# A two-layer decoder trunk in split fp32: gated blocks turned in two operations and moved by DMA, and a second seven-product step in gate/up tiles 3 to 9

## The reference

```python
def swiglu(h, w_gate, w_up, w_down):
    return (jax.nn.silu(h @ w_gate) * (h @ w_up)) @ w_down

for i in range(DEPTH):
    h = rms_norm(x, norm_mix[i])
    x = x + (gla_mixer(h, ...) if i % 2 == 0 else fox_mixer(h, ...))
    h = rms_norm(x, norm_ffn[i])
    x = x + swiglu(h, ffn_w_gate[i], ffn_w_up[i], ffn_w_down[i])
```

## Time and profile before

| | us |
|---|---|
| median of 3 runs | 2296.45 (2296.32 to 2296.54) |
| the profiled execution | 2296.2 |
| its span, first to last instruction | 2294.5 |
| PE busy in it | 2287.3 (10326 matmuls) |
| DVE busy | 1725.1 |
| ACT busy | 1153.3 |
| GpSimd busy | 167.1 |

### The profile page before, as it was taken

One profiled execution on the slowest core, in us unless ns is written; L12 is line 12 of the kernel. 1 busy time (PEld: TensorE's weight loads), 2 busy tenths in 40 slices (PEclk: granted clock), 3 DMA queues, 4 the chain that ended last, 5 costly groups with the idle time before them and its releaser, 6 DMA issues.

```text
span 2294.5 us, 28139 instructions
## 1 busy us (share of the span) xinstructions
PE 2287.3 (100%) x10326; PEld 1895.5 (83%) x10326; DVE 1725.1 (75%) x2151; ACT 1153.3 (50%) x1471; POOL 167.1 (7%) x206
## 2 busy tenths in 40 slices
PE   9999999999999999999999999999999999999999
PEld 7888788888888888888888888888888888888887
DVE  6888468678888887887578755577678888878575
ACT  5545554444445444454566656445444544545343
POOL 2036110000000000000222200001000000000000
PEclk9999999999999999999999999999999999999999
DMA  7655545666666666665768876656666666666664
GB/s 218 190 176 158 172 157 183 206 189 196 198 199 192 194 195 201 195 200 199 190 165 218 204 190 153 158 177 201 192 194 194 198 193 199 193 197 198 215 204 150
DMA packets 229950, 436.03 MB, mean 190 GB/s; under 512 B 17604, under 2 KB 19752, under 8 KB 229848
## 3 DMA queue, kind: packets, MB, share of 16 engines
q1 hardware_dynamic: 224416, 430.49, 63.7%
q0 software_dynamic: 1040, 3.69, 0.4%
q10 hardware_dynamic: 4392, 0.50, 0.2%
HBM read 432.52 MB, written 2.11 MB: 189 GB/s over the span
## 4 chain that ended last, share of the span: by engine, by line
PE 98%; DVE 1%; ACT 1%; issue 0%; ACTq 0%; POOL 0%; POOLq 0%; DVEq 0%
PE acc L418 16%; PE acc L420 16%; PE acc L419 16%; PE acc L428 14%; PE acc L429 14%; PE acc L427 14%; PE wk L646 1%; PE wk L428 1%; PE wk L427 1%; PE tp L428 1%; PE tp L427 1%; PE wk L429 1%; PE tp L429 1%; DVE w_lo L1244 0%; PE tp L385 0%; PE wk L703 0%
## 5 line engine op out<-in xcount | busy, mean ns | idle before, releaser
L766 ACT ACTIVATE w_hi<-raw 128x1024 fp32r<-128x1024 f32 x786 | 823.6, 1060 | 846.8 <-PE acc L429 451.5
L1244 DVE TENSOR_TENSOR w_lo<-raw,w_hi 128x1024 fp32r<-128x1024 f32 x786 | 971.7, 1250 | 367.7 <-ACT w_hi L766 363.3
L418 PE MATMUL acc<-w_hi,xt_hi 128*128 128x512 f32 x1408 | 554.3, 394 | 2.2 <-DVE w_lo L1244 2.1
L420 PE MATMUL acc<-w_hi,xt_lo 128*128 128x512 f32 x1408 | 548.3, 389 | 0.0
L419 PE MATMUL acc<-w_lo,xt_hi 128*128 128x512 f32 x1408 | 548.0, 389 | 0.0
L418 PEld LDWEIGHTS acc<-w_hi,xt_hi 128*128 128x128 f32 x1408 | 264.4, 188 | 60.5 <-issue 3.2
L427 PE MATMUL acc<-w_hi,xt_hi 128*128 128x512 f32 x798 | 310.4, 389 | 0.0
L428 PE MATMUL acc<-w_lo,xt_hi 128*128 128x512 f32 x798 | 310.4, 389 | 0.0
L429 PE MATMUL acc<-w_hi,xt_lo 128*128 128x512 f32 x798 | 310.4, 389 | 0.0
L420 PEld LDWEIGHTS acc<-w_hi,xt_lo 128*128 128x128 f32 x1408 | 264.3, 188 | 55.5
L419 PEld LDWEIGHTS acc<-w_lo,xt_hi 128*128 128x128 f32 x1408 | 264.5, 188 | 54.4 <-issue 1.0
(11 more groups left out here) (315 smaller groups left out, 1982.4 us busy)
## 6 DMA issues: line engine op xcount, KB each, us to landing
raw<-in_ffn_w_gate_dram SPq DMA_DIRECT2D x176, 512.0 KB, 4.2
raw<-in_ffn_w_up_dram SPq DMA_DIRECT2D x176, 512.0 KB, 4.2
raw<-in_ffn_w_down_dram SPq DMA_DIRECT2D x176, 512.0 KB, 4.3
raw<-in_fox_w_in_dram SPq DMA_DIRECT2D x128, 512.0 KB, 5.5
raw<-in_gla_w_in_dram SPq DMA_DIRECT2D x96, 512.0 KB, 4.5
raw<-in_gla_w_o_dram SPq DMA_DIRECT2D x32, 512.0 KB, 4.0
raw<-in_fox_w_o_dram SPq DMA_DIRECT2D x32, 512.0 KB, 4.1
xres<-in_x_dram SPq DMA_DIRECT2D x8, 256.0 KB, 6.6
```

The source lines that it names most:

```text
L418: pe.matmul(o, xh, wh, start=(k == 0), stop=False)
L420: last = pe.matmul(o, xl, wh, start=False, stop=(k == chunks * KC_CHUNK - 1))
L766: nc.scalar.activation(w_hi[:, slot, :], raw[:, slot, :], ACT.Copy).then_inc(hi_done, 1)
L1244: nc.vector.tensor_tensor(w_lo[:, slot, :], raw[:, slot, :], w_hi[:, slot, :].bitcast(F32), ALU.subtract).then_inc(lo_done, 1)
```

## The change

- `ORDER_GU` has two seven-product steps in each of the tiles 3 to 9: chunks 4 and 5 of the tile are the first, chunks 8 and 9 the second, with two ordinary gate chunks between. Before, the one step was chunks 6 and 7. The sums of x are made for two steps, with buffers twice as large; the products of both steps add up in the same PSUM banks.
- The gated block is turned by two DVE transposes (`squares_h`) of 128 partitions by 512 elements, after the fourth chunk. Each 32x32 square is turned where it stands, within its quadrant of partitions, into the memory of `act`. 16 DMAs of 32 partitions by 1 KB, issued by SP (`move`), then take the squares to their quadrants in `hraw`. SP's list has them after the eighth load of a tile, behind waits for the squares and for the readers of the last block.
- What reads `hraw` (the splits of the block, the sums for the down steps) has new access patterns, in runs of 32 elements, and waits for `moved`.
- The silu of a gate/up tile runs at the second chunk of the next tile instead of the end of its own; the joins stand at the last two chunks.

```diff
+    PAIRS = 2
+    GU = PAIRS * (GU1 - GU0)
+    ORDER_GU = [("one", 0, j) for j in range(2, 6)] + [("seven", 0, 0), ("seven", 1, 0), ("one", 0, 6), ("one", 0, 7),
+                                                       ("seven", 0, 1), ("seven", 1, 1)] \
+        + [("one", 1, j) for j in range(2, CH)]
...
+        ht_sq = act[:, :, :].rearrange("p b n -> p (b n)").rearrange("p (j f) -> p j f", j=4)
+        HQ = hraw[:, :, :].rearrange("p i (e c) -> p e i c", c=Q)
...
+                def move(t):
+
+                    n = g_up + t
+                    sp.wait_ge(turned, n + 1)
+                    sp.wait_ge(tp_hi, n)
+                    sp.wait_ge(tp_lo, n)
+                    if t == 0:
+                        sp.wait_ge(x_sum_raw, layer + 1)
+                    elif t <= SEVEN // 2:
+                        sp.wait_ge(sum_raw, layer * (SEVEN // 2) + t)
+                    for i in range(4):
+                        for j in range(4):
+                            sp.dma_start(hraw[Q * j:Q * j + Q, i, :], ht_sq[Q * i:Q * i + Q, j, :]) \
+                                .then_inc(moved, 16)
...
                     for n, (kind, t, j) in enumerate(ORDER_GU if GU0 <= i < GU1 else plain):
                         load((w_gate, w_up)[t][layer], j * KC_CHUNK * P, i * N, gate_chunk(c_up, i), n)
+                        if i and n == CH - 1:
+                            move(i - 1)
...
-                        wait(pe, diff_lo, step + 1)
+                        wait(pe, diff_lo, step + (j + 1))
...
-                    if n == 12:
-                        wait(ac, diff_used, gate_step(layer, i) + 1)
+                    if n == 1:
+                        silu()
+                    if n == 14:
+                        wait(ac, diff_used, gate_step(layer, i) + PAIRS)
                         nc.scalar.activation(g_sum[:, 0, :], seven_acc[0], ACT.Copy).then_inc(p1_gate, 1)
-                    if n == 14:
-                        silu()
                         turn()
...
+            def squares_h(n):
+
+                wait(ve, staged, n + 1)
+                dst = ht_sq.rearrange("p j (k b c) -> p b k j c", b=TB, c=Q)
+                for b in range(TB):
+                    last = nc.vector.transpose(dst[:, b], stage[:, b, :].rearrange("p (k j c) -> p k j c", j=4, c=Q))
+                last.then_inc(turned, 1)
...
-                        wait(ve, diff_used, step)
+                        wait(ve, diff_used, step + j)
...
-                    if n in (3, 4, 5, 8, 9, 10, 11, 12):
-                        swap(2 * (n - 3) if n < 6 else 2 * (n - 5))
-                    if n == 12:
+                    if n == 3:
+                        swap()
+                    if n == 14:
```

More of the change, by code:

```diff
@@ L351, in swiglu @@
                         load(w_down[layer], j * KC_CHUNK * P, i * (2 * N) + t * N, Lin(c_down + 2 * HCH * i), n)
+                        if i == 0 and n == CH - 1:
+                            move(FT - 1)
             def load_x(h):
@@ L478, in gate_up @@
[L478 to L481, removed]
+                        three(seven_acc[0], xt_hi[:, k, block0], xt_lo[:, k, block0], w_hi[:, a, upper],
+                              w_lo[:, a, upper], first, last)
@@ L873, in turn_x, with turn_h @@
                 last.then_inc(tp_hi, 1)
[L875 to L880, removed]
+            def turn_h(layer, n, t):
+                wait(ac, moved, (t + (layer * FT + 1)) * 256)
+                dst = ht_hi[:, bass.ds(t.v * 4, 4), :] if t.reg is not None else ht_hi[:, 4 * t.base:4 * t.base + 4, :]
+                nc.scalar.activation(dst.rearrange("p k (b i c) -> p (k b) i c", b=TB, c=Q), HQ,
+                                     ACT.Copy).then_inc(tp_hi, 1)
             def turn_y(n, t, gain):
@@ L926, in silu @@
                         ac.wait_ge(rstd_ready, norm + 1)
+                    wait(ac, moved, gate_tile(layer, i or 0) * 256)
                     for b in range(TB):
@@ L1307, in swap_h, with turn_h @@
                     last.then_inc(turned, 1)
-            def turn_h(n, t):
-                wait(ve, turned, n + 1)
+            def squares_h(n):
[4 more added lines that the diff above has]
+                last.then_inc(turned, 1)
+            def turn_h(layer, n, t):
+                wait(ve, moved, (t + (layer * FT + 1)) * 256)
@@ L1391, in gate_up @@
                                                 ALU.add).then_inc(gate_sums, 1)
-                    if n == 13:
+                    if n == 15:
+                        wait(ve, moved, gate_tile(layer, i) * 256)
                         wait(ve, gate_sums, sums + 1)
@@ L1568, in out_and_ffn @@
                     n = Lin(g_up - 1 + i)
-                    tile(cc, 0, lambda: hidden_joined(i) if i == GU1 else hidden(Lin(i - 1)), swaps=gate_swaps(n))
-                    tile(cc, CH, None, lambda: turn_h(n, Lin(i - 1)), swaps=up_swaps(n))
+                    tile(cc, 0, lambda: hidden_joined(i) if i == GU1 else hidden(Lin(i - 1)),
+                         swaps=squares(n))
+                    tile(cc, CH, None, lambda: turn_h(layer, n, Lin(i - 1)))
                 events = {}
```

138 lines of the change are left out of this document (72 added, 66 removed).

## The result

| | before | after |
|---|---|---|
| median | 2296.49 (2296.32 to 2296.90, 4 runs) | 2372.74 (2371.28 to 2374.29, 4 runs) |
| ratio, 95% interval | | 1.0333 (1.0320 to 1.0346) |
| span of the profiled execution | 2294.5 | 2371.4 |
| PE busy, matmuls | 2287.3, 10326 | 2307.1, 10284 |
| DVE busy | 1725.1 | 1654.8 |

The forecast was 2305.3, with a range up to 2322. The sign was right and the size was not: +76.2 us instead of +8.9.

What follows compares the result with a forecast made beforehand. The prediction took TensorE (PE), busy 2287.3 of 2294.5 us, as the bound. From 2296.2, -9.5 for matmuls removed and 12 x 1.5 + 2 x 0.3 of stalls gave +9.1: 2305.3 us, range 2286.5 to 2322.

Steps and rivals of the forecast that it cites:

- 9.5 us claimed: On PE, a second seven-product step in 7 tiles of 2 layers removes 42 matmuls, all on the path: 9.5 us.
- The squares: On DVE after the tile's fourth chunk: two wide transposes at 0.70 us each, done at T+5.43.
- rival (d): Wide squares cost 4 x 0.44 us each, so everything behind slides 2.1 us; about 2335 us, chance 0.04.
- The first step: At chunk 4: split differences end at T+12.38, PE wants them at T+12.92; no stall, by 0.3 us.
- The chain of the second step: At chunk 8: differences to low part, 6.95 us from T+15.94, ends T+22.89; PE wants it at T+23.12.
- the pitch of a move: On SP's queue after load 7: 0.44 us per move, 0.31 to 0.50 possible; 16 take 7.0 us.
- the landing: Loads 8 and 9 behind the moves: both landed 4.9 us after load 8's issue, 5.9 kept for the range.
- the granted clock: PE's clock in the stalls: assumed to stay at 1.00, a fall named only as a sign of being wrong.
- the forecast's 18.6 us of stalls: PE waits at the second step: 1.5 us in each of 12 tiles, 0.3 in each layer's first.
- (a): SP's issue is hidden: moves 0.34 us apart or less, no stall left; 2286.7 us, chance 0.16.
- (b): A balance: pitch 0.37 to 0.42 or quicker landings, stall eats the saving; 2291.5 to 2300.8 us, chance 0.24.
- (c): The forecast case: pitch 0.42 to 0.50, second landing 4.9 to 5.9; 2305.3 us, alone 2301 to 2320, chance 0.56.

Runs made afterwards that it cites:

- bounce: Changed kernel with the 16 moves replaced on SP by one DMA to device memory after load 7 and four back after load 11; 2286.99 us.
- pool: Changed kernel with the same 16 moves issued by GpSimd instead of SP; 2287.09 us.
- dram_moves: Changed kernel with all 16 moves on SP reading the same bytes from device memory instead of the squares; 2313.69 us.
- shapes: Changed kernel with four kinds of moves in successive tiles: unchanged, from device memory, 16 partitions, 128 partitions by 256 bytes; 2364.26 us, one run.
- spread: Changed kernel with the 16 moves still on SP, but two after each of loads 7 to 14; 2291.88 us.
- moves14: Changed kernel with 14 of the 16 moves, an eighth of the gated block being old data; 2342.99 us.
- two_steps: Changed kernel's new order of products with two seven-product steps, but turned by the 16 old transposes without DMAs; 2299.37 us.

## Why the prediction was wrong

**Right, with its numbers.** The 42 matmuls are worth 9.2 of the 9.5 us claimed (bounce). The squares cost 0.65 each in this tile (0.69 on average) for 0.70 assumed, and end at T+5.32 for T+5.43; rival (d) is out. The first step has no wait. The chain of the second step is 6.95, and the time for it is just enough: where loads are in time, PE releases the differences and no wait shows (pool, bounce). The mechanism was the forecast's: the moves hold SP, loads 8 and 9 are late, DVE's second differences are released by `raw`. The runs with 8, 12 and 14 moves, and those that spread the moves, join them or take them off SP, show it as the cause.

**The term that failed: the pitch of a move.** It was taken as 0.44, with bounds of 0.31 and 0.50, and is 0.63. That is 16 x 0.19 = 3.0 us in each tile, or 42.6 in all; with this term alone put right, the forecast's sum is 2347.9, already out of its range. The bounds came from the earlier trace rows; I had looked for rows near in size (partitions, bytes) and called 0.50 the most. All those DMAs read device memory. A move goes from SBUF to SBUF, and that is the property that counts: with device memory as its source the very same move has 0.46, close to my 0.44 (dram_moves). dram_moves is, so to say, the kernel that I had predicted: 2313.7, inside the range. It is still 8.4 above the forecast; 14 x 16 x 0.02 = 4.5 of these are the pitch and 1.1 the one fall of the clock, and the rest was not taken apart. I wrote that no row showed what a move costs, and then used the nearest rows as bounds all the same. None of those rows had both ends in SBUF, and so none could bound it.

The Trainium skill has two rules that bear on this, both in "DMA: Bandwidth & Descriptors", Rules for kernel authors. Small transfers are to be joined: the runs agree, as an issue cost the same with 16 partitions as with 32 (shapes), and five issues in place of sixteen gave the gain back (bounce). And to spread DMAs over SP, ACT and GpSimd is said to save issue time only, not bandwidth: here issue time was all there was to save, and it was worth 85.7 us, the way from 2372.7 to 2287.1 (pool).

**A smaller one: the landing.** I took 4.9 us from load 8's issue to the landing of both. By DVE's start it was 697.77 - 692.27 = 5.5. Of these 0.2 is that the first load behind the moves takes 0.58 to issue. The value was inside the bounds that I kept (4.9 to 5.9).

**In the tile shown:** the moves start at T+5.35 (5.5 assumed), chunk 9 is there at T+20.91 (17.4: -0.15 + 3.0 + 0.6), the low part is done at T+27.86 (24.4). At the full clock PE would have lost 4.9 us for 1.5.

**The term that was put at nothing: the granted clock.** I named its fall among the signs of being wrong and gave it no term, since it had stayed at 1.00 behind waits up to 1.0 us. The trace had no longer ones, and so said nothing of those. Behind the thirteen waits of over four us it fell to the level of 1.2 GHz each time, and that took 17.9 us: 26.3 lost behind the waits, less 14 x 0.6.

Together, against the forecast's 18.6 us of stalls: 14 x 3.04 = 42.6 from the pitch, 14 x 0.6 = 8.4 from the landing, -14 x 0.15 = -2.1 from the earlier start and 17.9 from the clock are 66.8; measured are 85.2 - 18.6 = 66.6. That it closes so well is partly luck, as three of the terms were read from one tile.

**The rivals.** (a), the hidden issue, and (b), the balance, asked for a pitch of 0.42 or less, which no kernel with the moves on SP had. (a)'s end did come out, 2287, in the kernels where the moves are elsewhere. (c) had the right mechanism, but the pitch lies outside its 0.42 to 0.50, and with it the time outside its upper end, 2319. Plain tiles and the start of the down phase were costed at nothing, and cost about 1 us in all in after. In spread, where the moves come later, they cost 4.8.

**What stays open.** Why a wait of 2.9 us brings the lower clock in one tile and not in the next. In moves14 those with it and those without mostly alternate, but no run was made for that. Nor do the runs say why an issue from SBUF to SBUF is dearer, what it would cost on ACT's queue, or why the old turning gives so little in two_steps.

## What to carry to other kernels

A queue that issues DMAs is an engine with a list of its own: for each issue that is added, ask what stands behind it and how long that can wait. Small DMAs belong on a queue whose next entry isn't urgent, or are joined into few; here both gave the whole gain (2287.0 and 2287.1, against 2296.1), while 16 issues ahead of two urgent loads turned a gain of 0.4% into a loss of 3.3%. The rows nearest in size bound the price of a DMA only if they have its kind of source and destination. And where PE waits for some us in every round of a loop, the wait isn't the whole price: the clock may drop behind it.

## What the runs showed of the hardware

- An issue of 512 KB on SP takes 0.37 us alone, be it a load or one from SBUF to device memory (bounce). One of 32 KB from device memory takes 0.33 alone and 0.42 in a series, and four of 128 KB took 0.47 each from start to start. From SBUF to SBUF it takes 0.51 alone and 0.59 in a series, whether 16, 32 or 128 partitions (0.60 there). The load right behind such a series took 0.58 in each of after's 22, and 0.42 behind a series from device memory (shapes).
- GpSimd issued the same moves at 0.50 each. They landed 3.4 us after their issue in the median, where SP's took 1.9 in after; nothing waited long for them.
- Transposes of 128 partitions by 512 elements take 0.69 on average, those of 32 by 256 take 0.44. Twice the elements and four times the partitions together cost 0.25 more; no row changes one of them alone. By form, in after (us busy, mean ns, idle before):

```profile
L1348 DVE STREAM_TRANSPOSE act<-stage 128x512 f32<-128x512 f32 x44 | 28.6, 687 | 0.0
```

- PE's granted clock fell from 2.4 to 1.2 GHz behind some waits from 2.0 us on and behind all of 3.7 and more. It stayed down for 5 to 7 matmuls with records of 0.63 us (11 to 13 in four cases) and cost about 1.1 us each time (some 2.3 in those four) beyond a wait without it.
